# Sharing on-chip buffers across the seams of projection, chunk stage and mixer, splitting part of the gates' weight earlier, and moving the first gate products beside the context

## The reference

```python
h_lat = modulate(rmsnorm(x, norm1_g), m_lat[0], m_lat[1])       # and h_ctx from ctx
z, xbc, dt_raw, q, k, v, g_out, gk_low = split(h @ w_in)        # the combined projection
xbc = silu(conv(xbc));  gf, gb = log_sigmoid(gk_low @ gk_up + bias) / 16
# SSD: 8 heads, chunks of 128;  GLA: 4 heads, chunks of 64 -- both forward and backward,
# latent scans start from the final context state of the same direction
y = rmsnorm((y_ssd + d_skip * x) * silu(z));  o = rmsnorm(o_gla) * silu(g_out)
x = x + m_lat[2] * (concat([y, o]) @ w_out)
# then RMSNorm, a top-2 mixture of 32 experts, gated residual, final RMSNorm
```

## Time and profile before

| | us |
|---|---|
| median of 3 runs | 2460.32 |
| the profiled execution's own time | 2460.65 |
| its span (first to last instruction) | 2458.5 |
| PE busy | 2166.5 (88%) |
| DVE busy | 1627.6 (66%) |
| ACT busy | 1136.0 (46%) |
| last instruction of the projection, first of the chunk stage | 602.4, 609.84 |
| last of the chunk stage (POOL's issue of a store aside), first of the mixer | 922.3, 928.88 |

### The profile page before, as it was taken

The page is one execution under the profiler, slowest core; times in us unless marked ns, Lnnn a source line. Parts: engine busy times, 40 slices in busy tenths (PEclk is TensorE's granted clock), DMA queues, the critical chain, the costliest instruction groups (busy, mean ns, idle before and its releaser), DMA issues. The chain is left out here.

```text
span 2458.5 us, 36215 instructions
## 1 busy us (share of the span) xinstructions
PE 2166.5 (88%) x11697; PEld 1710.4 (70%) x11697; DVE 1627.6 (66%) x2073; ACT 1136.0 (46%) x1469; POOL 532.0 (22%) x536
## 2 busy tenths in 40 slices
PE   4999999997799995999998039999999999999980
PEld 2777777775577774788887037787787788787760
DVE  1333333333566665677773529999999999999993
ACT  0222222222454542333332027777777777777762
POOL 1000000000000001232321433333333333333332
PEclk7999999998899995899999569999999999999995
DMA  8233333321877757889892615568988869989957
GB/s 312 73 112 111 112 123 119 121 103 59 284 277 284 286 216 278 300 301 308 291 298 73 233 46 159 154 207 264 291 282 270 256 206 351 318 280 323 360 195 290
DMA packets 210555, 548.61 MB, mean 223 GB/s; under 512 B 15232, under 2 KB 48507, under 8 KB 203291
## 3 DMA queue, kind: packets, MB, share of 16 engines
q1 hardware_dynamic: 180584, 443.11, 50.2%
q0 software_dynamic: 26224, 91.57, 14.8%
q10 hardware_dynamic: 3651, 12.65, 1.3%
HBM read 409.26 MB, written 138.01 MB: 223 GB/s over the span
## 5 line engine op out<-in xcount | busy, mean ns | idle before, releaser
L560 PE MATMUL pf<-hT,w_in_sb 128*128 128x256 f32 x1440 | 321.3, 386 | 1.1 <-DVE hT L641 1.1
L560 PEld LDWEIGHTS pf<-hT,w_in_sb 128*128 128x128 f32 x1440 | 278.9, 194 | 40.6 <-DVE hT L641 1.5
L2078 ACT ACTIVATE w_hi_e<-w_gates 128x2048 fp32r (+1 forms) x103 | 197.5, 1919 | 236.7 <-issue 103.3
L2204 DVE TENSOR_TENSOR w_lo_e<-w_gates,w_hi_e 128x2048 fp32r<-128x2048 f32 x103 | 236.4, 2296 | 33.2 <-ACT w_hi_e L2078 33.2
L2204 DVE TENSOR_TENSOR w_lo_e<-w_ups,w_hi_e 128x2048 fp32r<-128x2048 f32 x102 | 233.4, 2288 | 35.7 <-ACT w_hi_e L2078 35.7
L2204 DVE TENSOR_TENSOR w_lo_e<-w_downs,w_hi_e 128x2048 fp32r<-128x2048 f32 x100 | 228.3, 2283 | 0.0
L2078 ACT ACTIVATE w_hi_e<-w_ups 128x2048 fp32r (+1 forms) x102 | 195.2, 1913 | 23.6 <-PE pd_e L2151 22.4
L2078 ACT ACTIVATE w_hi_e<-w_downs 128x2048 fp32r x100 | 191.0, 1910 | 1.0
L2151 PE MATMUL pg_e<-w_hi_e,x_hi_e 128*128 128x512 f32 x408 | 167.1, 409 | 7.2 <-DVE w_lo_e L2204 7.2
L2056 POOL DMA_INDIRECT x_mid<-yb_e,to_e x50 | 126.9, 2538 | 185.2 <-DVE yb_e L2248 183.2
L2151 PE MATMUL pd_e<-w_hi_e,h_hi_e 128*128 128x512 f32 x400 | 162.1, 405 | 0.0
(11 more groups left out here) (374 smaller groups left out, 4486.0 us busy)
## 6 DMA issues: line engine op xcount, KB each, us to landing
w_gates<-in_w_gate_dram SPq DMA_DIRECT2D x32, 2048.0 KB, 12.1
w_ups<-in_w_up_dram SPq DMA_DIRECT2D x32, 2048.0 KB, 16.6
w_downs<-in_w_down_dram SPq DMA_DIRECT2D x32, 2048.0 KB, 10.2
tok_rec<-tm SPq DMA_DIRECT2D x9, 1936.0 KB, 7.2
rec_s<-tok_rec SPq DMA_DIRECT2D x18, 968.0 KB, 8.1
w_mod_half<-in_w_mod_dram SPq DMA_DIRECT2D x16, 1024.0 KB, 7.2
qk_rec<-qk_s SPq DMA_DIRECT2D x16, 1024.0 KB, 3.9
abc_m<-a_rows SPq DMA_DIRECT2D x16, 1024.0 KB, 4.9
```

The lines of the kernel that those rows point to most:

```text
L560: mm = pe.matmul(pf[n % 2][:, f, :], w[:, k, c0:c0 + P], h[:, k, :], start=(k == 0), stop=(k == KT - 1))
L2078: act.activation(w_hi[:, s % 3:s % 3 + 1, :], raw(part, half, place), ACT.Copy).then_inc(hi_done, 1)
L2204: dve.tensor_tensor(w_lo[:, s % 3:s % 3 + 1, :], raw(part, half, place), w_hi[:, s % 3:s % 3 + 1, :].bitcast(F32), ALU.subtract).then_inc( ...
```

## The change

Buffers: the chunk stage's three records, the decayed q/k, and from the chunk stage on `zg`, `fc` and the states are allocated outside of the stages and used by both neighbours. The projection writes the context's records and the last latent group's straight to where the chunk stage reads them. It no longer stores the context's records or the last `hT`, and does not wait for its last record store. The chunk stage no longer stores `qk`, `back_state`, `fwd_chunk` and `zg` of its last two tiles, which are the mixer's first two, and the mixer doesn't load them.

Weights of the gates: slices 0 to 2 are loaded, split and kept in the projection (after the groups 5, 6 and 7), the raw slices 3 to 5 are loaded there, and the exponential of `a_log` is taken there.

Order: the first latent tile's gate products stand between the products of the two context tiles, and the second tile's first half in the first's place, so that PE waits for the low parts slice by slice. `out_weight` comes ahead of `decayed_qk`. In the mixer ACT's loads of `w_gated` come first, and slices 0 to 3 are split ahead of the loop (ACT) and ahead of `gated_y(0)` (DVE).

```diff
 # build
+        recs = placed(spans, "right", "recs", 1, [P, 3 * T_LEN])[0]
+        raws = placed(early, "left", "raws", 1, [P, 3 * D + KT * GRP])[0]
...
+                slab += [t[:, 0:KT * MW].rearrange("p (k c) -> p k c", k=KT) for t in (raws, recs)]
 # projection
+        tm_ctx = [K["rec"][1][:, :], K["rec"][0][:, :]]
+        tm = [[flat[0], K["rec"][2][:, :]], [tm1[:, :], flat[1]]]
...
-                if not is_ctx:
+                if not is_ctx and after is not None:
                     sp.wait_ge(ht_done, it * 4 + 4)
                     sp.dma_start(ht_rec[it - 1], ...)
...
-                sp.wait_ge(tok_done, 2 * it + 2)
-                sp.wait_ge(g_done, it * 2 + 2)
-                sp.wait_ge(back_done, it * 4 + 4)
-                sp.dma_start(tok_g[it], tm[buf][:, :, :]).then_inc(stored[buf], 16)
+                if not is_ctx:
+                    for s in range(2):
...
+                        sp.dma_start(tok_g[it][:, s, :], tm[buf][s]).then_inc(stored[buf] if after is not None else K["last_stored"], 16)
+                if it == SPLIT - 1:
+                    for k in range(3):
+                        load_w(k)
+                if SPLIT <= it < LAT_GROUPS:
+                    sp.wait_ge(K["w_lo_done"], it - SPLIT + 1)
+                    load_w(it - SPLIT + 3)
...
+                if SPLIT <= it < LAT_GROUPS:
+                    k = it - SPLIT
+                    act.wait_ge(K["w_loaded"][k % 3], 32 * (k // 3 + 1))
+                    act.activation(w_hi[:, k, :, :], w_raw[k % 3][:, :, :], ACT.Copy).then_inc(K["w_hi_done"], 1)
 # chunks: SP
-            load(0)
-            for k in range(NW):
-                load_w(k)
-            load(1)
-            load(2)
-            load_ht(CT)
-            for k in range(NW, KT):
+            load(CT)
+            for k in range(KA + NW, KT):
                 sp.wait_ge(w_lo_done, k - NW + 1)
                 load_w(k)
+            sp.wait_ge(last_stored, 32)
 # chunks: ACT
+            features(CT)
+            weights(range(KA, KA + NW))
             for i in range(TILES):
                 exponentials(i)
-                if i < CT:
-                    weights(range(4 * i, 4 * i + 4))
+                if i == 0:
+                    weights(range(KA + NW, KT))
+                if i == CT - 1:
+                    features(CT + 1)
+                    gated(CT)
 # chunks: PE
-                    pe.wait_ge(w_lo_done, KT)
...
+                    if i == CT and n == 0:
+                        pe.wait_ge(w_lo_done, k + 1)
...
+            sums(0)
+            gate_product(CT, 0, z_ps)
+            sums(1)
+            pe.wait_ge(gate_done, 2)
+            products(0)
+            gate_product(CT, 1, g_ps)
+            products(1)
+            for i in range(CT, TILES):
                 sums(i)
                 if i == CT:
-                    pe.wait_ge(gate_done, 2)
-                if i >= CT:
+                    gate_product(i + 1, 0, z_ps)
+                elif i == CT + 1:
+                    gate_product(i, 1, g_ps)
+                else:
                     gate_product(i, 0, z_ps)
-                    scores(i)
+                scores(i)
                 products(i)
-                if i >= CT:
+                if i > CT + 1:
                     gate_product(i, 1, g_ps)
 # chunks: DVE
+            log_decays(0)
+            features(CT)
+            weights(range(KA, KA + NW))
...
                 weighted(i)
-                if i < CT:
-                    weights(range(4 * i, 4 * i + 4))
-                if CT <= i + 1 < TILES:
+                if i == 0:
+                    weights(range(KA + NW, KT))
+                if i == CT - 1:
+                    features(CT + 1)
+                if i > CT and i + 1 < TILES:
                     features(i + 1)
                 if i >= CT:
+                    out_weight(i - CT)
                     decayed_qk(i)
...
                     timed_scores(i)
-                    out_weight(i - CT)
 # mixer: SP, ACT, DVE
+                if t < 2:
+                    sp.dma_start(cT[b][:, :], feat_rec[t + CT][:, P:2 * P]).then_inc(front_loaded[b], 16)
+                    return
...
+            for k in range(NW):
+                load_w(k)
             decays(0, 0)
             decays(0, 1)
             inter_decays(0)
-            for k in range(NW):
+            weights(range(NW))
+            for k in range(NW, KT):
                 load_w(k)
...
+                if n == 0:
+                    weights(range(NW))
                 if before is not None:
                     split_m(before, 0)
...
                     gated_o(now)
-                if n == 0:
-                    weights(range(NW))
```

More of the change, by code:

```diff
@@ L154, in build @@
                 names = Names(nc, front, "frt")
-                slab = [front.enter_context(nc.sbuf_tensor(f"w_mod{b}", [P, KT, MW], F32)) for b in range(EARLY)]
+                slab = [front.enter_context(nc.sbuf_tensor(f"w_mod{b}", [P, KT, MW], F32)) for b in range(EARLY - 2)]
+                slab += [t[:, 0:KT * MW].rearrange("p (k c) -> p k c", k=KT) for t in (raws, recs)]
                 rows = front.enter_context(nc.sbuf_tensor("rows", [N_ROWS, P], F32))
@@ L472, in body @@
                     act.wait_ge(tok_ps, it * 2 + s + 1)
-                    if s == 0 and not is_ctx:
-                        act.wait_ge(stored[buf], use * 16 + 16 * buf)
-                    act.activation(tm[buf][:, s, T_V:T_V + GW], pz[s][:, :], ACT.Copy).then_inc(tok_done, 1)
+                    if s == 0 and not is_ctx and before_in(buf, use):
+                        act.wait_ge(stored[buf], before_in(buf, use))
+                    act.activation((tm_ctx if is_ctx else tm[buf])[s][:, T_V:T_V + GW], pz[s][:, :], ACT.Copy).then_inc(tok_done, 1)
                 for s in range(2):
@@ L489, in body @@
                     act.activation(soft[s][:, :], soft[s][:, :], ACT.Exp, scale=-1.0).then_inc(exp_done, 1)
+                if it == 1:
+                    act.wait_ge(a_loaded, 32)
+                    act.activation(K["nega"][:, :], K["nega"][:, :], ACT.Exp).then_inc(a_exp, 1)
                 for s in range(2):
@@ L760, in chunks @@
         grow = [sb(f"grow{b}", [P, 4, P]) for b in range(2)]
-        qk = [sb(f"qk{b}", [P, 4, 4, P]) for b in range(2)]
         scm, back_sc = sb("scm", [P, 2, 2, P]), sb("back_sc", [P, SH, P])
@@ L769, in chunks @@
         pzg = [ps("pz"), ps("pg")]
-        w_loaded = [sem(f"w{b}_loaded") for b in range(NW)]
+        w_loaded, w_hi_done, w_lo_done, last_stored = (K[n] for n in ("w_loaded", "w_hi_done", "w_lo_done", "last_stored"))
         rec_loaded = [sem(f"rec{b}_loaded") for b in range(NR)]
@@ L870, in _ @@
         def _(act):
-            act.wait_ge(a_loaded, 32)
-            act.activation(nega[:, :], nega[:, :], ACT.Exp).then_inc(a_exp, 1)
             def weights(ks):
@@ L988, in gate_product @@
                 for k in range(KT):
-                    for j, (a, w) in enumerate(((hi, w_hi), (hi, w_lo), (lo, w_hi))):
-                        mm = pe.matmul(pzg[n][:, :], a[:, k, :], w[:, k, n, :], start=(k == 0 and j == 0), stop=(k == KT - 1 and j == 2))
+                    if i == CT and n == 0:
+                        pe.wait_ge(w_lo_done, k + 1)
+                    for j, (a, w) in enumerate(((hi, w_his), (hi, w_los), (lo, w_his))):
+                        mm = pe.matmul(pzg[n][:, :], a[:, k, :], half(w, k)[:, n, :], start=(k == 0 and j == 0), stop=(k == KT - 1 and j == 2))
                 mm.then_inc(done, 1)
@@ L1135, in out_weight @@
                                          op0=ALU.mult, op1=ALU.mult).then_inc(wo_gated, 1)
-            for n in range(2):
+            log_decays(0)
+            features(CT)
+            weights(range(KA, KA + NW))
+            for n, src in enumerate((early, late)):
                 dve.wait_ge(gate_ps, n + 1)
-                dve.tensor_copy(gate_bc[:, 512 * n:512 * n + 512], pzg[n][:, :]).then_inc(gate_done, 1)
-            log_decays(0)
+                dve.tensor_copy(gate_bc[:, 512 * n:512 * n + 512], src[:, :]).then_inc(gate_done, 1)
             for i in range(TILES):
@@ L1270, in _ @@
             load(0)
-            load_zg(0)
+            load(1)
             for n in range(LT):
@@ L1275, in _ @@
                     load_abc(n + 1)
-                    load(n + 1)
-                    load_zg(n + 1)
+                    if n:
+                        load(n + 1)
+                        load_zg(n + 1)
                 if n + 1 < LT:
```

221 lines of the change are left out of this document (134 added, 87 removed).

## The result

The changed kernel takes 2427.02 us (median of 4 runs, 2423.26 to 2428.52), the kernel before 2459.91 (4 runs, 2458.32 to 2461.0): ratio 0.9862, 95% interval 0.9848 to 0.9876. That is 32.9 us less, against 39.3 forecast; the median lies inside the range, 6 us above the forecast. "Gain" is how much earlier a moment comes than before.

What follows compares the result with a forecast made beforehand. PE's start of unbroken work was taken as the bound, with idle time at the stage seams; 27.6 + 7.4 + 4.8 - 0.5 = 39.3 us off 2460.65 gave 2421.4, forecast 2421, range 2414 to 2433.

Steps and rivals of the forecast that it cites:

- First seam: Projection to chunk stage: waiting only for the last record store's issue starts the chunk stage at about 604.0; 5.8 us.
- Context stretch: Chunk stage's start to third latent tile's `sums`: PE nearly unbroken, `sums` at 653.5 instead of 681.1; 27.6 us including first seam.
- the floor of 47.8 us: Context stretch: PE's own work before the third latent tile's `sums`, without waits, 47.8 us.
- Rival 1: Context: PE's half clock lasts or last slices come late, 5 to 11 us lost, 2426 to 2432; chance 0.20.
- rival 3: Context: moved gate work pushes the context's own chain back; only the seams gain, 13 us, 2447; chance 0.06.
- 17.0 us per tile after it: Chunk stage from the third latent tile's `sums` on: each tile takes 17.0 us; over 17.1 would show the forecast wrong.
- Second seam: Chunk stage to mixer: without the last tiles' stores the mixer starts 1.6 us after ACT's SiLU, at 921.5; 7.4 us.
- Mixer's start: Mixer's first DVE chain, on which `ssd(1)` hangs, ends 40.8 us after the start against 45.6; 4.8 us, bounds 0.8 and 6.8.
- d: Mixer's start: delay of context loads by ACT's `w_gated` loads, taken as 2 us, between 0 and 6.
- rival 2: Mixer's start: 2.1 MB of `w_gated` go first, delay 6 us, 4 us lost, 2425; chance 0.68 together with the forecast.
- Rival 4: Chunk stage: moved `out_weight` overruns the store-and-load ring through `wo_raw`, 50 us lost, kernel takes 2471; chance 0.03.
- The end: Program's end: clearing the shared semaphores, one more clearing and barrier, costs 0.5 us (bounds 0 and 1.6).

Runs made afterwards that it cites:

- both later profiles of the changed kernel: The changed kernel unchanged, timed again in the first and third follow-up studies: 2424.13 and 2423.48 us.
- the two doubled pieces: Changed kernel with output-weight pieces of tiles 3 and 4 put off, two taken a tile in tiles 8 and 12: 2430.47 us.

## Why the prediction was right, and where it was off

- **First seam**: 5.8 forecast, 5.8 found; the chunk stage starts at 604.08 (604.0). Undoing it alone costs 5.0; what the other 0.8 are is open. The splits put into the projection, costed at nothing, cost nothing in this pair of profiles.
- **Context stretch**: the floor of 47.8 us met PE's 47.84 busy us, in part by luck: spreading the gate took 3.4 us, not 3.8, and some work behind it ran at half clock instead. Waits for low parts were 0.2 + 0.9 = 1.1 us (forecast 0.6), none for `xw` (0.3), and the clock was 0.97 over the stretch. The forecast 1.7 us of losses are 1.2 measured, and `sums` of the third latent tile began at 653.04 (653.5). Rival 1 (cold or late) didn't occur, nor rival 3 (only the seams). Yet 2427 us is a time that rival 1 gave, 2426 to 2432. The upper part of the range was there for rival 1 alone, and other losses, which no rival named, filled it. That the range held is in that measure luck; the mechanism of seams and context is not.
- **"17.0 us per tile after it": the step that failed.** I carried the 27.6 us unchanged through the stage, since each engine's order in later tiles is that of before. It is not in one: between tile 3, whose `pg` had been taken early, and tile 4, which follows the old pattern, PE has 3.0 us of work over a DVE and ACT chain of 5.3. The chain was in the trace of the kernel before (in one tile copies from 694.52 us, table load at 695.48, SiLU at 696.77 and 698.30), but not in the rows that I read. 4.2 us lost, 2.5 as a wait and 1.5 as half clock behind it, repeated in both later profiles of the changed kernel. A tile of more than 17.1 us was one of the prediction's own signs of being wrong. Removing the wait alone gave nothing, and the two changes of ACT's order gave back 2.1, so half of the 4.2 has its cause shown by an edit; the other half is read from the traces.
- **Second seam**: 8.0 us against 7.4: a seam with nothing to land cost 0.98 us here, not 1.6.
- **Mixer's start**: mis-sized by 2.1 us, 2.7 against 4.8 (it comes to 45.70 - 42.99 us), and the point named as a sign of error, a first segment later than 18 us, was passed. d, taken as 2, is 6.8 - 4.1 = 2.7; holding the loads gave 2.6 back, so this term is shown. Another 1.4 us is `po_m` at half clock (3.46 for 2.05 us), for which the prediction had no term; in the third profile of the changed kernel it took 1.87 us and `ssd(1)` came after 41.5 us, not 43.0. What decides the clock there is open: with the loads held it was still at half. From the first segment on DVE took 940.12 - 916.25 = 23.9 us, exactly the 23.9 of the forecast.
- **Which loads go first**: the landings, 6.3 against 3.7 us with and without the second queue's 2.1 MB, don't fit weights first, which would have cost 6 us (rival 2). The Trainium skill ("DMA: Bandwidth & Descriptors", Queues, rings and completion order) has each DMA engine take turns between its queues packet by packet. By that rule d is an estimated 2.2 us. The traces agree with it roughly: d was 2.7, and the second load landed 2.6 us later.
- **Rival 4, the ring through `wo_raw`**, showed once: DVE waited 2.36 us for it, until 667.09, and PE was busy all that time. In all other tiles there is no such wait. When the ring was really overrun (the two doubled pieces) each cost 3 to 4 us, so its mechanism exists and its condition doesn't hold.
- **The end**: experts' start 33.5, whole execution 32.1. Forecast were 0.5 us for the clearing; 0.9 us more goes between the mixer's second `ssd` and the experts' first matmul, and 1.4 behind that. Most of this is scatter of one execution. From `ssd(1)` to the experts it is 463.2 us before and 464.2 here, but 462.1 to 463.5 in the twelve profiles of the experiments. From there to the span's end it is 1020.7 before and 1022.5 here, but 1020.9 to 1021.7 in the twelve. Their mean over both parts is 0.3 us above the kernel before, of which there is one profile, so that the clearing costs 0.5 is neither shown nor refuted.

Sum of the misses: 4.2 - 0.5 (context) + 0.1 (later tiles) in the chunk stage, -0.6 at the second seam, 2.1 in the mixer, 1.8 behind: 7.1, and 39.3 - 32.1 = 7.2 but for rounding.

## What to carry to other kernels

When work is moved out of its place in a steady loop, check not only the place where it goes but the first ordinary iteration behind it: what the moved work used to cover (here the 5.3 us in which DVE and ACT free a product's buffer) lies bare there once. Before giving a freed wait its full price, list which chains end within 2 or 3 us behind it: here taking away one wait (2.47 us) gave nothing, and two together 2.1 of 4.2. And where a stage's start has a small load on the critical path, hold back large loads of other queues until it has landed; one line brought the mixer's second `ssd` 2.6 us nearer to the stage's start, and 2.9 and 1.5 in two other pairs of profiles.

## What the runs showed of the hardware

- From 652 to 670 us the DMA share is 1.0 at 342 to 407 GB/s. The short tile ahead (641.51 to 653.04) moved 2.4 MB, the third latent tile 7.4, and a tile of 17.0 us in the kernel before 4.8: the bytes of the short tile fall into the next. The loads issued there take 8.7 us (record) and 9.2 us (features), which is no more than the same loads took in tiles of 17.0 us (8.5 and 9.5 in the kernel before, 690 to 730 us). What the short tiles changed is the time that is there to cover them.
- An 8 KB store's issue took 3.30 us on SP's queue at 653.81 in that stretch and 2.06 and 1.26 in the next two tiles; from 700 us on 0.32, but for one of 0.89.
- A wait of 2.47 us was followed by a gate half of 7.27 us in one execution and of 5.77 in another with the same wait: the granted clock over it was 0.76 in the one and 1.00 in the other. Of eight profiles with this wait the clock fell in seven, of two with the wait for `cz` in one. An estimate of such a pause should carry both.
- After a doubled turn of the ring, a load issued behind a store made DVE wait 7.2 and 6.3 us, where 5 were expected.
